# One-hot rows of the first keys: stored once and loaded for three expert blocks instead of compared anew

## What is computed

```python
cand_i = (i1[..., :, None] * PEER_KEYS + i2[..., None, :]).reshape(t, PEER_HEADS, -1)
top_s, pos = lax.top_k(cand_s, PEER_TOPK)
expert = jnp.take_along_axis(cand_i, pos, axis=-1).reshape(t, -1)
gate = jax.nn.softmax(top_s, axis=-1).reshape(t, -1)
z = jnp.einsum('cd,ced->ce', xc, u[ec])
act = jax.nn.gelu(z, approximate=False) * gc
out = jnp.einsum('ce,ced->cd', act, v[ec])
```

## Time and profile before

| | us |
|---|---|
| three runs | 3145.31, 3151.75, 6184.49 |
| their median | 3151.75 |
| the profiled execution | 3146.41 |
| its span on the core | 3144.4 |
| mean granted clock of PE | 0.996 of 2.4 GHz |
| DVE busy | 2407.6 |
| ACT busy | 1743.9 |

### The profile page before, as it was taken

One profiled execution on the slowest core, in us unless ns is written; L12 is line 12 of the kernel. 1 busy time (PEld: TensorE's weight loads), 2 busy tenths in 40 slices (PEclk: granted clock), 3 DMA queues, 4 the chain that ended last, 5 costly groups with the idle time before them and its releaser, 6 DMA issues.

```text
span 3144.4 us, 62060 instructions
## 1 busy us (share of the span) xinstructions
PE 3106.8 (99%) x24748; PEld 3003.6 (96%) x24748; DVE 2407.6 (77%) x3908; ACT 1743.9 (55%) x2400; POOL 308.2 (10%) x303
## 2 busy tenths in 40 slices
PE   9999999999999999999999999999999999999998
PEld 9999999999999999999999988999999999999997
DVE  8767777755556776666668999988799789988887
ACT  6444545777776655555655455554555545554454
POOL 2000000000000000000000022331133112210110
PEclk9999999999999999999999999999999999999999
DMA  5444435444444545555455555678867787665785
GB/s 203 147 160 148 169 115 211 161 169 163 160 164 171 185 168 182 176 180 177 164 188 180 185 199 202 245 264 287 297 236 251 274 287 249 244 214 188 259 291 194
DMA packets 117821, 637.37 MB, mean 203 GB/s; under 512 B 11633, under 2 KB 32497, under 8 KB 50417
## 3 DMA queue, kind: packets, MB, share of 16 engines
q1 hardware_dynamic: 98496, 565.49, 50.7%
q0 software_dynamic: 18864, 68.43, 6.7%
q10 hardware_dynamic: 288, 1.05, 0.1%
HBM read 632.57 MB, written 2.36 MB: 202 GB/s over the span
## 4 chain that ended last, share of the span: by engine, by line
PE 86%; DVE 8%; DVEq 2%; ACT 2%; DMA 1%; issue 1%; ACTq 0%; SPq 0%
PE bank L670 14%; PE bank L672 14%; PE bank L671 14%; PE bank L1153 11%; PE bank L1206 9%; PE bank L1154 5%; PE bank L1207 5%; DVE wl L1856 3%; PE bank L1196 2%; PE bank L1198 2%; PE bank L1197 2%; PE bank L1117 1%; PE bank L824 1%; PE bank L1156 1%; ACT wh L1344 1%
## 5 line engine op out<-in xcount | busy, mean ns | idle before, releaser
L1856 DVE TENSOR_TENSOR wl<-raw,wh 128x1024 fp32r<-128x1024 f32 x1052 | 1267.1, 1238 | 349.9 <-ACT wh L1344 341.1
L1344 ACT ACTIVATE wh<-raw 128x1024 fp32r<-128x1024 f32 x1052 | 1052.7, 1050 | 394.3 <-DMA raw<-w_in_a 128.6
L671 PE MATMUL bank<-hhl,wh 128*128 128x256 f32 x3568 | 989.1, 277 | 0.0
L670 PE MATMUL bank<-hhl,wh 128*128 128x256 f32 x3440 | 966.9, 281 | 1.0 <-DVE hhl L1904 1.0
L672 PE MATMUL bank<-hhl,wl 128*128 128x256 f32 x3440 | 953.4, 277 | 0.0
L671 PEld LDWEIGHTS bank<-hhl,wh 128*128 128x128 f32 x3568 | 673.4, 189 | 1.9 <-issue 1.7
L670 PEld LDWEIGHTS bank<-hhl,wh 128*128 128x128 f32 x3440 | 647.9, 188 | 5.1 <-issue 2.4
L672 PEld LDWEIGHTS bank<-hhl,wl 128*128 128x128 f32 x3440 | 647.2, 188 | 0.0
L1153 PE MATMUL bank<-hhl,wh 128*128 128x448 f32 x1920 | 625.0, 382 | 6.8 <-DVE wl L1856 6.7
L1154 PE MATMUL bank<-hhl,wl 128*128 128x224 f32 x2048 | 522.4, 265 | 0.0
L1206 PE MATMUL bank<-ahl,wh 128*128 128x448 f32 x1488 | 472.1, 374 | 2.4 <-DVE ahl L2570 2.1
(11 more groups left out here) (461 smaller groups left out, 4405.2 us busy)
## 6 DMA issues: line engine op xcount, KB each, us to landing
raw<-peer_u SPq DMA_DIRECT2D x128, 1024.0 KB
raw<-peer_v SPq DMA_DIRECT2D x128, 1024.0 KB
raw<-w_in_c SPq DMA_DIRECT2D x64, 1024.0 KB
raw<-w_in_a SPq DMA_DIRECT2D x63, 1024.0 KB
raw<-w_kv SPq DMA_DIRECT2D x32, 1024.0 KB
raw<-w_in_b SPq DMA_DIRECT2D x32, 1024.0 KB
raw<-w_out_a SPq DMA_DIRECT2D x16, 1024.0 KB
raw<-w_out_b SPq DMA_DIRECT2D x16, 1024.0 KB
```

Of the source, the lines that this page charges most:

```text
L670: eng.matmul(out, h_[:, k, :], high[:, k, :], start=(k == 0), stop=False)
L671: eng.matmul(out, h_[:, k, :], low[:, k, :], start=False, stop=False)
L1344: eng.activation(high_half(c, half), raw_half(c, half), ACT.Copy).then_inc(hi_ready, 1)
L1856: eng.tensor_tensor(low_half_out(c, half), raw_half(c, half), high_half(c, half).bitcast(F32), ALU.subtract).then_inc(lo_ready, 1)
```

## The change

A tensor in the chip's memory, hot_rows_of, holds 28 tiles of hot_a. In U1 DVE makes hot_a as before, and SP stores each tile behind the weight loads. In U2, U3 and V2 DVE no longer makes hot_a: SP loads tile n-2 behind the weight load of unit n (for turns 0 and 1 of a block: at the end of the block before that used hot_a), and PE waits for it (hot_in). In U1 DVE waits for the store of tile n-2 before it writes tile n into the same buffer (hot_stored). SP's code of these four blocks is unrolled. To free four semaphores, waits of stage X share two counters (css_step, kw_step) in place of one semaphore for each step; the order of that stage is the same. Cut to its core:

```diff
+        hot_stored = [sem(f"hot_stored{n}") for n in range(2)]
+        hot_in = [sem(f"hot_in{n}") for n in range(2)]
...
+        hot_rows_of = nc.dram_tensor("hot_rows_of", (TURNS, P, TG * P), F16, kind="Internal").ap()
...
+            def store_hot(n):
+
+                eng.wait_ge(sQ["pairs_ready"], n + 1)
+                eng.sem_inc(sp_passed, 1)
+                eng.dma_start(hot_rows_of[n], hot_tile(n)).then_inc(hot_stored[n % 2], 16)
+
+            def load_hot(b, n):
+
+                if (b, n) == (1, 0):
+                    for k in range(2):
+                        eng.wait_ge(hot_stored[k], 16 * (TURNS // 2))
+                eng.wait_ge(sQ["g_done"], b * TURNS + n - 1)
+                eng.sem_inc(sp_passed, 1)
+                eng.dma_start(hot_tile(n), hot_rows_of[n]).then_inc(hot_in[n % 2], 16)
+
+            def block_with_hot(name, table, b):
+
+                last = BLOCKS - 1 if name == "V" else b - 1
+                for n in range(BJ):
+                    load(n // PER_PAIR, BASE[f"{name}{b}"] + n % PER_PAIR, one(table, b * BJ + n))
+                    if 2 <= n < TURNS + 2 and last == 0:
+                        store_hot(n - 2)
+                    elif 4 <= n < TURNS + 2:
+                        load_hot(last, n - 2)
+                    elif TURNS + 2 <= n < TURNS + 4 and last < BLOCKS - 1:
+                        load_hot(last + 1, n - 2 - TURNS)
...
-                block_of(name, peer_u if name == "U" else peer_v, b)
+                if name == "U" and b > 0 or (name, b) == ("V", PAIRED):
+                    block_with_hot(name, peer_u if name == "U" else peer_v, b)
+                else:
+                    block_of(name, peer_u if name == "U" else peer_v, b)
...
                 eng.wait_ge(s["pairs_ready"], n + 1)
+                if b > 0:
+                    eng.wait_ge(hot_in[c % 2], i * (16 * PER_PAIR // 2) + 16 * (((b - 1) * TURNS + c) // 2 + 1))
...
-                eng.tensor_tensor(hot_a[c % 2][:, :, :, :], iota_h[:, :, :].unsqueeze(1).broadcast_to(ka),
-                                  token_pairs[:, 0].unsqueeze(2).broadcast_to(ka), ALU.is_equal)
+                if b == 0:
+                    if n > 1:
+                        eng.wait_ge(hot_stored[c % 2], 16 * (n // 2))
+                    eng.tensor_tensor(hot_a[c % 2][:, :, :, :], iota_h[:, :, :].unsqueeze(1).broadcast_to(ka),
+                                      token_pairs[:, 0].unsqueeze(2).broadcast_to(ka), ALU.is_equal)
```

More of the change, by code:

```diff
@@ L554, in _, with hot_tile @@
             row("Q", w_q, KC)
+            def hot_tile(n):
+                return hot_a[n % 2][:, :, :, :].rearrange("p a k two -> p (a k two)")
+            def store_hot(n):
[19 more added lines that the diff above has]
+                        load_hot(last + 1, n - 2 - TURNS)
             def block_of(name, table, b):
@@ L982, in _ @@
                 if g == 0:
-                    eng.wait_ge(s["kn_ready"], 1)
+                    eng.wait_ge(s["kw_step"], 6)
                     for t in range(NT):
                         last = eng.transpose(B[5][:, t * P:(t + 1) * P], kdup[:, t].rearrange("p a d -> p (a d)"), ident[:, :])
-                    last.then_inc(s["kt_done"], 1)
+                    last.then_inc(s["kw_step"], 1)
                 if g == 1:
-                    eng.wait_ge(s["kt_ready"], 1)
+                    eng.wait_ge(s["kw_step"], 8)
                 if g >= 1:
@@ L1633, in _ @@
                     high_part(0, u + 5)
-            last.then_inc(s["csq_ready"], 1)
+            last.then_inc(s["css_step"], 1)
             high_part(0, u + 6)
             eng.wait_ge(mm_done, 2 * (u + RC + 1))
-            eng.activation(kw_fm, B[2][:, 0:T], ACT.Copy).then_inc(s["kwf_ready"], 1)
+            eng.activation(kw_fm, B[2][:, 0:T], ACT.Copy).then_inc(s["kw_step"], 1)
             high_part(0, u + 7)
-            eng.wait_ge(s["kwt_done"], 1)
+            eng.wait_ge(s["kw_step"], 2)
             eng.activation(kw[:, :, :], B[5][:, 0:NT * P].rearrange("p (t n) -> p t n", t=NT)[:, :, 0:IDX_DIM + IDX_HEADS],
[L1641 to L1645, removed]
+                           ACT.Copy).then_inc(s["kw_step"], 1)
+            eng.wait_ge(s["css_step"], 3)
+            rsqrt(crs[:, :], crs[:, :], 1.0 / KV_RANK, None).then_inc(s["css_step"], 1)
+            eng.wait_ge(s["kw_step"], 4)
             for t in range(NT):
@@ L2282, in _ @@
                 low_part(0, u + c)
-            eng.wait_ge(s["css_done"], 1)
-            eng.tensor_tensor(crs[:, :], B[4][:, 0:T], epsv_c[:, :], ALU.add).then_inc(s["cvar_ready"], 1)
-            eng.wait_ge(s["kw_ready"], 1)
+            eng.wait_ge(s["css_step"], 2)
+            eng.tensor_tensor(crs[:, :], B[4][:, 0:T], epsv_c[:, :], ALU.add).then_inc(s["css_step"], 1)
+            eng.wait_ge(s["kw_step"], 3)
             for t in range(NT):
@@ L2300, in _ @@
             last.then_inc(s["ckv_ready"], 1)
-            eng.wait_ge(s["krs_ready"], 1)
+            eng.wait_ge(s["kw_step"], 5)
             for t in range(NT):
@@ L2304, in _ @@
                     last = eng.tensor_scalar(kdup[:, t, a, :], kc[:, t, :], kst[:, 2, t:t + 1], None, ALU.mult)
-            last.then_inc(s["kn_ready"], 1)
+            last.then_inc(s["kw_step"], 1)
             eng.memset(iscore[:, :], 0.0)
```

22 lines of the change are left out of this document (11 added, 11 removed).

## The result

The changed kernel takes 3201.73 us (median of 4 runs, 3192.09 to 3204.43), the kernel before 3150.88 us in runs beside it (median of 4; one of them took 6184.49 us and moves the median by under 1 us): a ratio of 1.0162, 95% interval 1.0132 to 1.0191. It is 51 us slower, inside the forecast's range and 10 us above its 3192. The profiled execution took 3201.7 us.

A forecast was written before the change was run, and what follows sets the result against it. PE, busy 3106.8 of 3144.4 us, was taken as the bound; waits for hot tiles add 39 us in U2 and U3 and 5 in V2, together 44: 3190 us profiled, about 3192 median, range 3155 to 3245.

The forecast's parts named there:

- The compare on DVE: U2, U3, V2: removing 84 compares takes 57 us off DVE, worth 0 because PE is never idle there.
- The stores in U1: U1: SP's 28 stores of 256 KB have 9.2 us to land, so they cost 0, at most 5 us.
- The time there is and the time it takes: U2, U3, V2: tile needs 5.65 us, has 5.01 (U) or 5.28 (V2); late by 0.6 or 0.4 us.
- The stall at every second turn: U2, U3, V2: a stall gives the next tile more time, so PE stalls in 13 pairs of turns a block.
- What makes up the 1.5: U2, U3: a pair of turns costs 0.6 us clean, 2.5 beside a fetched row; 1.5 taken, 39 us in both.
- Its sign for the rows: U2, U3: with DVE earlier, a row's fetch begins more than 2.8 us ahead of the weight load.
- V2: 13 x 0.4 = 5 us: V2: with few fetched rows, each of 13 pairs of turns costs 0.4 us, 5 us in all.
- From the sum to the median: Whole kernel: profiled 3146.4 + 44 = 3190 us, expected as about 3192 for the median of runs.
- In time: Rival, U2, U3, V2: tiles land within the unit, 8 us at most, 3146 to 3160; in time or nearly, chance 0.23.
- By DVE: Rival: DVE really paces PE's products, so its 57 us show, down to 3089 us; faster 0.05, over 2% 0.01.
- The clock falls: Rival: stalls of about 2 us halve PE's clock, 3226 to 3260 us; contended or clock drops, over 63 us, chance 0.22.
- list of signs that it was wrong: No PE waits for hot_a, waits at every turn, granted clock below 1.00 in these blocks, or U1 longer.

The follow-up runs named there:

- e3_no_compare: Kernel before the change, with DVE's compare that makes hot_a left out in U2, U3 and V2, nothing put in its place: 3147.84 us, ratio 0.9999.
- e2_same_moment: Changed kernel, with the hot tile's load issued at the same moment as the weight load but in front of it: 3150.11 us, ratio 1.0005.
- e4_v2_by_dve: Changed kernel, but in V2 DVE makes hot_a again, with no load or wait there: 3184.78 us, ratio 1.0109.
- e6_more_ahead: Changed kernel, with a 256 KB copy issued between weight load and hot load, SP first waiting for the previous copy: 3274.34 us, ratio 1.0392.

## Why the prediction was right, and where it was not

**The compare on DVE: 57 us off DVE, worth 0.** Right: 57.1 us, and e3_no_compare measures the worth at 0.9999 (0.9988 to 1.0009). The bound of 2 us gained at block ends is within that interval.

**The stores in U1: 0, up to 5.** Right: PE 151.50 of 151.50 us. SP itself waited 65 us there for tiles to be ready, ahead of its stores, and PE felt none of it. The margin was thinner than the forecast had it: the stores whose landing the trace gives (14 of 28) took 3.7 to 8.9 us, where 7.6 was the longest it reckoned with and 9.2 us were there.

**The time there is and the time it takes.** Forecast: the clean tile lands 5.65 us after the weight's issue. Measured: issued 0.43 after it and landed 5.1 to 5.2 later, 5.5 to 5.6. In the U blocks a turn whose tile has nothing beside it costs 0.4 us on average (7 turns, 2.7 us in all), in V2, whose unit is 2809.66 - 2803.97 = 5.69 us, next to nothing (8 turns, 0.1 us). The forecast had 0.6 and 0.4. The difference is SP's issue, which the unrolled code brought 0.16 us forward (0.25 us behind PE's start in a turn without a wait, 0.41 before); the forecast named that gain and then did not use it. e2_same_moment shows that its reason, the megabyte ahead in the same queue, is the right one.

**The stall at every second turn.** Right as an average of the U blocks only: 30 waits in the 52 turns of U2 and U3 that could wait, and 10 in the 26 of V2. They do not alternate strictly: in U2 turns 6 and 7, 9 and 10, 12 and 13, 15 and 16 wait in a row, a short wait (0.2 to 0.35 us) and then a long one, as a short stall gives the next tile only that much more time. U2 and U3 cost 37.0 us (38.4 again) where 39 were forecast, 1.42 us a pair for 1.5.

**What makes up the 1.5.** Wrong in part. The forecast had clean stalls of 0.6 us and stalls of 2.5 us behind a fetched row. The table of landings shows that a row alone leaves the median at 5.11 us (4 of 29 over 5.5). The long stalls stand beside packets of instructions, which the forecast did not look at although the page of before lists their queue, and mostly where a row is there too; and 6 us of the 37 are the clock, which the forecast had only in a rival. That the price came right is in part luck: the 10 late weight loads of the earlier trace rows were ascribed to only a part of the traffic (in U2 and U3 of after, 10 weight loads took over 5.8 us, 9 of them beside a row and a q8 packet and one beside a row alone), the clean stall was set too high, and the half-clock spells filled the sum. Its sign for the rows held: a fetch now begins 3.95 us ahead of the next weight load at the median in U2, against 2.3 before.

**V2: 13 x 0.4 = 5 us.** The term that was mis-sized: 16.6 and 13.0 us, and by e4_v2_by_dve 16. The step that failed is "V2, with few rows", which priced every pair as clean. V2 has no rows for most of it but the most instruction packets, 12 in its 28 turns against 7 in U2, and 11 tiles there landed beside a q8 packet and no row, up to 6.8 us. The units whose tile landed beside such a packet have 14.5 of V2's 16.6 us (0.7 of it in the first unit, whose tile was early). Over the three blocks 44 us were forecast and 53.6 measured, and this term is more than the whole difference.

**From the sum to the median.** The 3192 does not follow from its own terms: 44 us on the median of 3151.75 is 3196, and measured from the kernel before in the same runs it is 44 against 51 us.

**The rivals.** "In time" was closer than it looks: e2_same_moment is in time with the same traffic and the same moment, by the order of two lines. "By DVE" is out by e3. "The clock falls" happened in part: 20.5 us at half clock, some 10 us of the 54, with a mean granted clock of 0.98 in the three blocks. A granted clock below 1.00 in these blocks stood in the forecast's list of signs that it was wrong, so by its own list that one came true; and the landings that it expected at 5.5 to 7.5 us after issue were 5.0 to 8.5, median 5.2. In e6_more_ahead it took over, at a tile 2.0 us later and a mean wait of 1.9 us; the forecast had put the point of decision at stalls of about 2 us.

## What to carry to other kernels

Before a value is stored and loaded again to spare an engine, ask whether that engine is waited for at all (here 57 us of it were worth nothing), and how long the new load has between its release and its use. A small load inherits the place at which it stands in its queue: behind a 1 MB load of the same moment it took 5.2 us, in front of it 2.8, and a unit ahead it did not matter; code that issues loads in order should issue the one that is due first, first. A margin of a few tenths of a microsecond against a landing is no margin, since single landings run to 8 us, and a stall of some 2 us or more may cost 1.5 more by the clock.

## What was not expected of the hardware

- 16 KB packets of instructions (q8), 0.9 to 1.9 us each in these blocks, stand beside 17 of the 23 hot tiles that landed more than 5.5 us after issue; the same tile with nothing beside it never took over 5.26 us in the profile of after. 1 MB weight loads with no other traffic beside them took 5.30 us at the median when such a packet began 0.5 to 3.5 us after their issue (56 loads of ten traces), against 4.90 without. Packets of 8 KB on q14, which carry SP's and POOL's code, made little difference when added.
- A fetched row of 512 KB on another queue, 0.23 MB of it within the time of a hot tile's landing, left that landing at 5.1 us; with more than 0.3 MB of a row beside it and no instruction packet the median was 5.36.
- 96 semaphore increments on POOL take about 15 us, 0.15 us each.
- After a stall of 3.67 us the clock was 1.2 GHz for 3.4 us only, which cost 1.5 us beyond the stall; e6_more_ahead, with 88.6 us of waits at the small products, spent 68 us at half clock.
